# Two-layer diffusion backbone on one core: the first modulation in column chunks, and the first head's decay exponentials behind the q and k copies

## What is computed

```python
sh1, sc1, g1, sh2, sc2, g2 = split(silu(c) @ w_ada[l] + b_ada[l], 6)   # c: one vector for each of two streams
hm = rmsnorm(x, norm_pre_mix[l]) * (1 + sc1) + sh1
rq, rk, rv, rg, nq, nk, nv = split(hm @ w_in[l])                     # rq, rk: 4 heads of 128
y, s_f, s_b = retention_bidir(rope(rq), rope(rk) * k_scale, rv, log_sigmoid(decay_logit[l]), s0_f, s0_b)
# decay inside a chunk: exp(log_gamma * distance); xi and zeta: exp(log_gamma * position)
```

## Time and profile before

| what | us |
|---|---|
| median of 3 executions | 2200.7 (2197.87 to 2201.38) |
| the profiled execution, own time | 2201.11 |
| its span in the trace | 2199.3 |
| PE busy | 2126.4 |
| DVE busy | 1548.2 |
| ACT busy | 924.9 |

### The profile page before, as it was taken

The page is one execution under the profiler, slowest core; times in us unless marked ns, Lnnn a source line. Parts: engine busy times, 40 slices in busy tenths (PEclk is TensorE's granted clock), DMA queues, the critical chain, the costliest instruction groups (busy, mean ns, idle before and its releaser), DMA issues. The chain is left out here.

```text
span 2199.3 us, 34007 instructions
## 1 busy us (share of the span) xinstructions
PE 2126.4 (97%) x14016; PEld 2021.5 (92%) x14016; DVE 1548.2 (70%) x2467; ACT 924.9 (42%) x1478; POOL 111.5 (5%) x208
## 2 busy tenths in 40 slices
PE   5999999999999999999979999999999999999997
PEld 3999999999978999999879999999998899999996
DVE  5687767477756887887777776655854558787885
ACT  4555432476234433333365554225743434333332
POOL 1000010110100000000000000001100000000000
PEclk9999999999999999999999999999999999999998
DMA  6333244324444222222323333432234312222223
GB/s 277 121 116 116 89 166 144 104 91 151 126 106 163 67 77 96 77 77 96 142 110 115 115 115 115 168 130 77 83 116 102 148 51 85 77 77 95 78 77 134
DMA packets 62890, 245.94 MB, mean 112 GB/s; under 512 B 8080, under 2 KB 8112, under 8 KB 60176
## 3 DMA queue, kind: packets, MB, share of 16 engines
q1 hardware_dynamic: 41040, 153.12, 21.0%
q0 software_dynamic: 21696, 90.65, 11.7%
HBM read 230.08 MB, written 13.66 MB: 111 GB/s over the span
## 5 line engine op out<-in xcount | busy, mean ns | idle before, releaser
L1520 DVE TENSOR_TENSOR wl<-raw,wh 128x1024 fp32r<-128x1024 f32 x204 | 246.6, 1221 | 159.0 <-ACT wh L1097 156.9
L483 PE MATMUL unit<-hmh,wh 128*128 128x320 f32 x1152 | 347.4, 309 | 1.4 <-DVE sig L2005 1.1
L484 PE MATMUL unit<-hml,wh 128*128 128x320 f32 x1152 | 346.7, 309 | 0.0
L486 PE MATMUL unit<-hmh,wl 128*128 128x320 f32 x1152 | 262.5, 309 | 0.0
L1097 ACT ACTIVATE wh<-raw 128x1024 fp32r<-128x1024 f32 x204 | 209.5, 1050 | 120.8 <-DMA raw<-w_main 120.8
L1622 DVE CUSTOM_DVE_ANT_0 junk<-ada,csb,par 128x1024 f32<-128x1024 f32 x160 | 205.5, 1285 | 30.5 <-DMA ada<-w_ada 10.3
L483 PEld LDWEIGHTS unit<-hmh,wh 128*128 128x128 f32 x1152 | 216.5, 188 | 2.1 <-issue 1.9
L484 PEld LDWEIGHTS unit<-hml,wh 128*128 128x128 f32 x1152 | 216.4, 188 | 0.2
L471 PE MATMUL unit<-wh,hmh 128*128 128x256 f32 (+1 forms) x640 | 202.3, 316 | 7.5 <-DVE t L1546 3.8
L473 PE MATMUL unit<-wh,hml 128*128 128x256 f32 (+1 forms) x640 | 200.7, 314 | 0.0
L472 PE MATMUL unit<-wl,hmh 128*128 128x256 f32 (+1 forms) x640 | 200.4, 313 | 0.0
(11 more groups left out here) (448 smaller groups left out, 5258.6 us busy)
## 6 DMA issues: line engine op xcount, KB each, us to landing
raw<-w_main SPq DMA_DIRECT2D x276, 512.0 KB, 3.8
ada<-w_ada POOLq DMA_DIRECT2D x80, 512.0 KB, 4.4
first<-w_first SPq DMA_DIRECT2D x8, 1024.0 KB, 18.8
x<-x_keep POOLq DMA_DIRECT2D x3, 2560.0 KB, 9.4
bias<-biases POOLq DMA_DIRECT2D x32, 192.0 KB, 2.7
x<-x POOLq DMA_DIRECT2D x2, 2560.0 KB, 11.4
x_keep<-x POOLq DMA_DIRECT2D x10, 512.0 KB, 2.9
bias<-biases POOLq DMA_DIRECT2D x16, 256.0 KB, 4.2
```

The source lines that it names most:

```text
L483: pe.matmul(u[:, h, 0:n], a[0], xs[h][0], start=f, stop=False)
L484: pe.matmul(u[:, h, 0:n], a[0], xs[h][1], start=False, stop=False)
L486: mm = pe.matmul(u[:, h, 0:n], a[1], xs[h][0], start=False, stop=z)
L1520: dve.tensor_tensor(wl[slot[i]][:, :], raw[slot[i]][:, :], f32(wh[slot[i]][:, :]), ALU.subtract)\
```

## The change

1. `w_first` is cut by output columns: piece c has all 1024 input rows, and the 128 columns of sh1 chunk c and of sc1 chunk c. `cc` is padded with zeros to 32 columns a chunk, and PE sums a piece by 8 matmuls of 256 columns in four column groups of 32 rows (input chunk k in group k % 4). ACT copies all 128 rows to one of two `mrows`; two matmuls against a constant selection matrix (two new columns of `zpos`) add the groups and turn the result to columns; DVE makes `mod`, `am1` and z of that chunk alone. PE's two columns of `w_in` run three chunks behind the sums, between them.
2. x is loaded first, in two transfers on SP's queue, and the first two slabs come after the second piece; POOL's queue keeps the small tables. All five tiles of x are turned before the first sums. The copies of a turned tile stand between the norms of later ones. The four splits of this stage stand inside the chunk loop at c = 1, 2, 6 and 7. `decays` comes behind the copies.
3. In head 0 of each layer the decay exponentials on ACT stand behind the copies and swaps of q and k; in all heads DVE's wait for them, with the two additions of the identity to `dst`, stands behind `kl`.

```diff
+            def first_sums(c):
+                pe.wait_ge(first_in[c], 16)
+                if c == 0:
+                    pe.wait_ge(tr_free, TILES)
+                    pe.wait_ge(zv_ready, TILES)
+                if c >= 2:
+                    pe.wait_ge(rows_ready, c - 1)
+                for k in range(KD):
+                    g = k % 4 * 32
+                    mm = pe.matmul(sc[c % 2][g:g + 32, 0:2 * P], cc[:, k, :], wf[c][:, k, :], start=k < 4, stop=k >= 4)
+                mm.then_inc(sums_ready, 1)
+            def turn_rows(c):
+                pe.wait_ge(rows_ready, c + 1)
+                if c >= 2:
+                    pe.wait_ge(first_mod, c - 1)
+                for a in range(2):
+                    mm = pe.matmul(tp[c % 2][:, 2 * a:2 * a + 2], mrows[c % 2][:, a * P:(a + 1) * P], zpos[:, 8:10], start=True, stop=True)
+                mm.then_inc(turned, 1)
...
+            for c in range(KD + 3):
+                if c < KD:
+                    first_sums(c)
+                if 1 <= c <= KD:
+                    turn_rows(c - 1)
+                if c == 3:
+                    for _ in range(2):
+                        w, _, _ = slab(P)
+                        units.append((U.take(), w))
+                        U.add()
+                if c >= 3:
+                    k = c - 3
                     pe.wait_ge(hm0_ready, k + 1)
                     for u, w in units:
...
             sp.dma_start(cc[:, :, :], ccol).then_inc(cv_load, 16)
-            for k in range(KD):
-                if k == KD - 1:
+            for i, ts in enumerate((slice(0, 2), slice(2, TILES))):
+                sp.dma_start(x[:, ts, :], x_in[:, ts, :]).then_inc(x_part[i], 16)
+            for c in range(KD):
+                if c == 2:
                     for i in range(2):
                         weights(i)
-                sp.dma_start(wf[k][:, :], w_first[k]).then_inc(first_in[k], 16)
+                sp.dma_start(wf[c][:, :, :], w_first[c]).then_inc(first_in[c], 16)
...
+            for c in range(KD + 1):
+                if c < KD:
+                    act.wait_ge(sums_ready, c + 1)
+                    if c >= 2:
+                        act.wait_ge(turned, c - 1)
+                    act.activation(mrows[c % 2][:, :], sc[c % 2][:, 0:2 * P], ACT.Copy).then_inc(rows_ready, 1)
+                if c >= 1:
+                    act.wait_ge(z_ready, c)
+                    act.activation(hmh[:, c - 1, :], xt[:, c - 1, :], ACT.Copy).then_inc(zh_ready, 1)
+                if c in (1, 2, 6, 7):
+                    split()
...
+                    if h:
+                        exponentials()
                     if h:
                         head_root()
                     for n, (to, sw, scale) in enumerate(((qs, qsw, 1.0), (ks, ksw, K_SCALE))):
...
+                    if h == 0:
+                        exponentials()
                     for n, (to, of) in enumerate(((qh, qs), (kh, ks))):
...
                         lo(to[:, :], of[:, :], hi[:, :]).then_inc(qk_ready, 1)
 
+                    dve.wait_ge(dexp_ready, heads.count + 1)
+
+                    for at_ in (DIAG, CTX_DIAG):
+                        dve.tensor_tensor(dst[:, at_:at_ + P], dst[:, at_:at_ + P], ident[:, :], ALU.add)
```

More of the change, by code:

```diff
@@ L168, in build @@
         epsc = fixed("epsc", [P, 1])
-        cc = fixed("cc", [P, KD, 2])
+        cc = at("cc", [P, KD, 32], csb_at)
+        mrows = [at(f"mrows{i}", [P, 2 * P], csb_at + KD * 32 * 4 + i * 2 * P * 4) for i in range(2)]
         flag = fixed("flag", [P, 1])
@@ L571, in _ @@
-            mm.then_inc(sums_ready, 1)
-            for half in range(2):
-                pe.wait_ge(rows_1, half + 1)
-                if half:
-                    pe.wait_ge(rows_2, 1)
-                for c in range(KD * half, KD * half + KD):
-                    rows = slice(c // 4 * 32, c // 4 * 32 + 2)
-                    mm = pe.transpose(unit[1 - half][:, c // 4 % 2, c % 4 * 2:c % 4 * 2 + 2], mrows[rows, c % 4 * P:(c % 4 + 1) * P], ident[rows, rows])
-            mm.then_inc(turned, 1)
@@ L581, in two_columns @@
-            def two_columns():
-                units = []
-                for _ in range(2):
-                    w, _, _ = slab(P)
-                    units.append((U.take(), w))
-                    U.add()
-                for k in range(KD):
+            def first_sums(c):
[9 more added lines that the diff above has]
+                mm.then_inc(sums_ready, 1)
@@ new lines, in turn_rows @@
+            def turn_rows(c):
[5 more added lines that the diff above has]
+                mm.then_inc(turned, 1)
+            pe.wait_ge(early_in, EARLY)
+            for _ in range(TILES):
+                turn_tile()
+            pe.wait_ge(cc_ready, 1)
@@ L594, in two_columns @@
                             mm.then_inc(unit_ready, 1)
-                for n in range(2):
-                    slab_done.append((unit_ready, U.count - 1 + n))
+            for n in range(2):
+                slab_done.append((unit_ready, U.count - 1 + n))
             for l in range(DEPTH):
@@ L1138, in _, with features_first @@
             act.wait_ge(const_set, 1)
[L1139 to L1146 removed]
+            def features_first(t):
                 act.wait_ge(tr_ready, t + 1)
@@ L1696, in _ @@
                 if c < KD:
+                    both = slice(SH1 + c, SC1 + c + 1, KD)
+                    dve.wait_ge(turned, c + 1)
+                    dve.tensor_tensor(mod[:, 0, both, :], tp[c % 2][:, 0:4].rearrange("p (a n) -> p a n", a=2),
+                                      par[:, 0, B_ADA + SH1 + c:B_ADA + SC1 + c + 1:KD].unsqueeze(2).broadcast_to([P, 2, 2]), ALU.add)\
+                       .then_inc(first_mod, 1)
+                    dve.drain()
+                    dve.scalar_tensor_tensor(out=am1[:, 0, c, :], in0=mod[:, 0, SC1 + c, :], scalar=1.0,
+                                             in1=par[:, 0, N_PRE_MIX + c:N_PRE_MIX + c + 1].broadcast_to([P, 2]), op0=ALU.add, op1=ALU.mult)
+                    dve.drain()
                     for i, cols in STREAMS:
@@ L1717, in _ @@
                         head_stats()
-                    dve.wait_ge(dexp_ready, heads.count + 1)
-                    for at_ in (DIAG, CTX_DIAG):
-                        dve.tensor_tensor(dst[:, at_:at_ + P], dst[:, at_:at_ + P], ident[:, :], ALU.add)
                     if h:
```

104 lines of the change are left out of this document (41 added, 63 removed).

## The result

The changed kernel takes 2208.3 us in the median (seven runs, 2205.4 to 2213.1), the kernel before, run beside it, 2199.5 us (seven runs, 2195.7 to 2202.5): ratio 1.0041, 95% interval 1.0029 to 1.0054. It is slower by 8.8 us where the forecast was no measurable change, and 2208.3 lies above the range (2196.5 to 2206.5). The profiled execution has a span of 2207.2 us, 7.9 more than before.

The account below looks back on a forecast made before the run. PE, busy for 97% of the span, was taken to bound the kernel. -2.2 + 0 + 3.3 = +1.1 us on the profiled 2201.11 gave 2202.2, forecast as 2202.0 us since that execution lies 0.4 over the median; range 2196.5 to 2206.5.

Parts of the forecast that it names:

- Product 0 at 31.4: Kernel start: PE's first product of the two columns starts at 31.4 us, 9.6 us earlier than 40.97.
- the -2.2 us: Kernel start: the values start at 55.7 us in place of 57.93, 2.2 us earlier.
- From product 0 to the values 24.3 us: Column stage on PE: products 14.1 us, sums 4.0, turnings 2.3, half clock 2.6, waits 1.3.
- The rival of sums that do not overlap: Column stage: only two groups run side by side, a group of sums takes 2.1 us; 2206.9 us, chance 0.10.
- The tile-mode rival: Column stage: PE drains at each change between column groups, 0.27 us each, +2.7 us more; 2204.9 us, chance 0.08.
- First head of the first layer: 0, bound 0.5: First layer: late exponentials delay the `vl` chain by 1.1 us, hidden by 2.7 us to spare; zero, upper bound 0.5.
- the condition I gave: First layer: hidden unless the slab ACT splits between q and k comes over 1.5 us later, beside `csb`'s load.
- Second layer's first head: +3.3: Second layer: late exponentials delay `kl`, `dst` and `vl`; 1.95 us lost plus 1.35 for slow clock; bounds -1.35 to +4.8.
- the 1.35 gained: Second layer's first head: PE no longer waits 1.35 us for ACT's q copy behind the exponentials.
- the Trainium skill's 2.66: Second layer's table load: the page's price of 2.66 us per switch gives +4.7 there, 2203.4 in all; chance 0.05.
- The rest of the kernel: a plain shift, as long as nothing behind it comes late: Behind the start of the values: the end moves by as much as that start, if nothing later comes late.

Follow-up runs that it names:

- in the gap: Changed kernel with a first head's exponentials between the copy of k and the slab's split: 2202.8 us, ratio 1.0031.
- late in first alone: Changed kernel with late exponentials in the first layer only, the second layer's ahead of the q copy again: 2202.3 us, ratio 1.0030.
- early writes: Second layer's small `g_rows` writes issued during attention: in before 2204.7 us (1.0037), in the changed kernel 2211.4 (1.0068), in late in first alone 2206.2 (1.0043).
- changed with early writes: Changed kernel with the second layer's small `g_rows` writes issued during attention: 2211.4 us, ratio 1.0068.
- old places: Changed kernel with 32 unused bytes, so that tiles lie in SBUF where they lay before: 2206.6 us, ratio 1.0043.
- narrow `ccol`: Changed kernel with c's columns narrow in HBM as before and zeros filled in SBUF: 2206.0 us, ratio 1.0043.
- Start alone: Changed kernel with the exponentials and DVE's wait for them back in their old places: 2200.7 us, ratio 1.0027.
- exponentials alone: Kernel before with only the late exponentials, and DVE's wait and additions behind `kl`: 2198.8 us, ratio 1.0013.
- decays in the loop: Decay-rate chain moved behind chunk 2: in the changed kernel 2201.9 us (1.0027), in late in first alone 2198.3 (1.0013).
- experiment 4: For a later start: kernel before with extra ACT copies delaying it, 2197.6 us (1.0004); the same delay in exponentials alone, 2200.3 (1.0017).
- x in two: Kernel before with x loaded by SP's queue in two transfers, as the changed kernel loads it: 2199.0 us, ratio 1.0007.
- x by SP in one: Kernel before with x loaded in one transfer by SP's queue in place of POOL's: 2195.6 us, ratio 0.9993.
- wide inputs: Kernel before with the two inputs padded in HBM as in the changed kernel, the same numbers read: 2198.8 us, ratio 1.0014.
- longer code: Kernel before with 80 tiny unused matmuls more on PE at the start: 2199.6 us, ratio 1.0013.

## Why the prediction was wrong, step by step

- *Product 0 at 31.4.* Failed, and with it the -2.2 us: 33.03, the values at 57.5. Late by 1.6: the second part of x at 10.78 (forecast 9.8), the first tile not turned before 10.83, since it waits for the last of POOL's small tables, `zpos`, a wait that I had left out; ACT stands idle 0.28 us for that part of x and 0.58 us for that tile, the last copy on DVE ends at 20.2 (forecast 18.7), and `decays` at 25.2 in place of 23.8. Over the seven profiles with the changed kernel's start (changed, in the gap, late in first alone with and without early writes, changed with early writes, old places, narrow `ccol`: 57.4 to 59.4) V is 58.1 in the mean, against 57.6 in seven with the old start undelayed and TensorE's code as it was: +0.5 where -2.2 was summed. (Start alone is left out: its 60.5 has the wait for q's copy.) I had named `decays` as what sets this point and not asked whether it had to stand there.
- *From product 0 to the values 24.3 us.* 24.45 in this profile, partly by luck, and 25.0 in the mean of the seven (24.4 to 25.6). Sums took 1.07 us a group (0.99 from start to start), the turning 0.47 from its start to the next product (forecast 0.45), the wait for `hml` 1.05 in place of 1.3. The half clock lasted only from 33.03 to about 36.5 and so cost 1.7 us in place of 2.6; the eight products took the difference, 1.92 us each in place of 1.76. The rival of sums that do not overlap fell. The tile-mode rival fell too: the turning starts at 23.73 where the sums' row runs to 23.80, and from the last matmul of a product to the first of the sums it is 0.24 us (39.67 to 39.91) where two matmuls of a product are 0.15 apart, so that this change costs some 0.1 us and not 0.27.
- *First head of the first layer: 0, bound 0.5.* Too small: A is 237.8 us in the mean of nine profiles with late exponentials behind the new start, and 236.4 with late exponentials behind the old one, +1.4. In the changed kernel the slab lands at 62.86, 2.2 us later than before, and PE waits 0.74 us for `vl`; the condition I gave (the slab over 1.5 us late beside `csb`) was met. That slab takes 6.1 to 6.7 us from issue to landing in all ten profiles with the new start and 3.4 to 3.6 in all ten with the old one. Start alone has the late slab too, without late exponentials, and its A is 236.6: the 1.4 us need both. That `csb` delays the slab was not tried by itself.
- *Second layer's first head: +3.3.* Right in mechanism, and in size within its bounds (up to 4.8), though not sharply measured. By pairs of ratios: 2.9 us (exponentials alone against before), 2.4 (changed against late in first alone), 3.1 (the two with decays in the loop), 5.5 (the two with early writes). By the maps B is 249.8 us in the mean of the six with late exponentials in this layer (in the gap left out) and 245.7 in the ten without, +4.1. In the changed kernel's profile it was +5.3: the wait for `vl` was 2.8 us (forecast 3.0), and the q copy no longer kept PE, but the values started at 1141.38 where they had started at 1141.45, since the half clock lasted longer (below), so that the 1.35 gained was missing. The table load again has 1.28 us in its row and `dst` follows at once: the Trainium skill's 2.66 (ScalarE: Activation LUTs, What ACT_TABLE_LOAD costs) does not show here.
- *The rest of the kernel: a plain shift, as long as nothing behind it comes late.* Failed: I put that condition at nothing without a reason. Something does come late. A later start alone is a plain shift (experiment 4), but in the profiles with x in two transfers by SP the weight slab amid the small writes near 1680 us lands some 3 us later, and C is 3.2 us longer, 1.6 ms after the edit.

So three terms of the sum were off: the start (-2.2, measured +0.5), the first layer's head (0, measured +1.4) and the rest (0, measured +3.2). With the second layer's head at 3 us, as three of the four pairs of ratios have it, the terms give +0.5 + 1.4 + 3 + 3.2 = 8.1 us, with the maps' 4.1 they give 9.2, against 8.8 measured. Shown by experiment: that the late exponentials cost the second layer some 3 us or more, and that the decay chain set product 0. Supported, not shown: the two transfers as the cause of the 3.2. X in two against x by SP in one is 3 us in ratio, 1.0007 against 0.9993, with intervals that overlap a little; but x in two is not clearly slower than before itself, and two edits of no visible effect (wide inputs, longer code) measured about 3 us too. Open: why the place in a queue should delay a slab so late. Decays in the loop, with the values 2.8 us early, still ends 5.9 us behind before; stand, A and second head give 7.6 to 8.7 less 2.8, that is 4.8 to 5.9.

## What to carry to other kernels

When a long wait is removed, list all that it hid, on every engine: here 5 us of small vector operations became the limit, while the same engine idled for as long one step later, and moving them there gave back 3 to 4 us. Here, work moved behind a copy was paid for where the next buffer is released, not where the copy was. And when a change's parts are measured alone, compare stage by stage over several profiles: two profiles of the same kernel differed by 5.4 us here.

## What the runs showed of the hardware

**The clock after one and the same wait.** Before the second layer's columns PE waits 3.05 us, behind the turning of five tiles, in all three kernels shown here. Windows of the changed kernel, of exponentials alone, and the second window of before (length, PE, PEld, DVE, ACT and POOL busy, granted clock, DMA share, GB/s):

```profile
1132.80:1135.50 2.70, 2.68 (x12) 2.68 (x13) 2.60 (x3) 1.59 (x2) 1.60 (x3) 0.50 0.28 121
1135.50:1138.20 2.70, 2.70 (x15) 2.70 (x14) 1.48 (x3) 0.00 (x0) 0.00 (x0) 0.50 1.19 485
1138.20:1141.40 3.20, 3.20 (x26) 3.20 (x26) 0.84 (x2) 2.03 (x4) 0.00 (x0) 0.87 1.00 307
```

```profile
1132.80:1135.50 2.70, 2.51 (x21) 2.51 (x22) 2.59 (x4) 1.76 (x2) 1.60 (x3) 1.00 0.29 121
1135.50:1138.20 2.70, 2.70 (x25) 2.70 (x24) 1.65 (x3) 1.89 (x4) 0.00 (x0) 1.00 0.98 394
```

```profile
1135.50:1138.20 2.70, 2.70 (x24) 2.70 (x23) 1.50 (x3) 1.06 (x1) 0.00 (x0) 0.97 1.19 485
```

Before had 0.50 for the first of these stretches only the earlier trace rows. After the same wait the clock was at 1.2 GHz for 2.7 us (before), for over 5.4 (changed), or not at all (exponentials alone), and from the first product to the values it took 8.6 (with the 1.35 us wait for q), 8.6 (without it) and 5.85 us.

**Scattered small writes.** Over the 17 profiles that issue them near 1680 us, POOL waited 16.1 to 19.2 us, from the end of their issue, until the last of four transfers of 4 KB in 4-byte pieces had landed. A slab of 512 KB issued amid them took 11.8 to 18.3 us to land and kept ACT waiting for 8.9 to 15.4 us. The same slab in the three kernels with early writes took 3.4 to 3.6 us; in the changed kernel with early writes:

```profile
raw<-w_main SPq DMA_DIRECT2D x1, 512.0 KB, 3.6
```
